# Attention scores of a sliding-window layer: a head's query stacked as high over low part in 128 rows, the key stored twice, two matrix products in place of three; and another order of the Vector engine's work at a group's last step

## The chip, the cores and the metric

One core of one Trainium2 chip runs the whole program. The metric is the device time of one execution in microseconds, from its first to its last instruction and the little that lies around them. Engines are named as in the profile: PE is the Tensor engine (PEld its weight loads), DVE the Vector engine, ACT the Scalar engine, POOL the GpSimd engine, SP the engine that issues the DMAs. Each works through a queue of its own in order, and they wait for each other by semaphores.

## What is computed

Two layers of a decoder trunk on 1024 tokens of width 1024, all in float32: layer 0 mixes by retention, layer 1 by sliding-window attention, and each is followed by a squared-ReLU MLP. The change touches the attention alone:

```python
q = rope(rmsnorm(q.reshape(b, s, 16, 64), q_gain), positions)     # 16 query heads
k = rope(rmsnorm(k.reshape(b, s, 4, 64), k_gain), positions)      # 4 key heads
kb = with_prev(k)      # per block of 128 queries: the block before and this one, 256 keys
scores = jnp.einsum("bnqkgd,bnskd->bnkgqs", qb, kb) * 64 ** -0.5
scores = jnp.where(mask, scores, -jnp.inf)
probs = softmax(concat([scores, sink]))[..., :-1]
o = jnp.einsum("bnkgqs,bnskd->bnqkgd", probs, vb)
return o.reshape(b, s, 16 * 64) @ w_out
```

## The kernel before

**Precision.** A float32 product is made of three fast ones. Each operand is split into a high part (a copy rounded to `float32r`, made on ACT) and a low part (operand minus high part, made on DVE), and `product` (lines 528 to 538) issues high x high, high x low and low x high. In the profile these three are L533, L534 and L535. A name with `_hi` or `_lo` is such a part.

**Order of the program.** Retention, its output projection, the MLP of layer 0, the attention (about 1.5 to 1.9 ms into the trace), and the MLP of layer 1. The order on every engine is written out by hand.

**The attention.** It is 4 groups (one key head and its four query heads each) of 8 steps (`TT`, one block of 128 tokens each), 32 steps. `sw_steps` writes for each engine what it does in a step `s` of a group `g`. Group 0 and group 3 are written out, groups 1 and 2 are the two turns of a hardware loop (`Fori`), and two draining steps follow. The block `i` passes through the stages in three successive steps:

- `a_pe`: projection of the block to 384 columns (256 query, 64 key, 64 value), 24 matmuls. ACT squares it (`sq_act`, L2274) and copies it (`copy_act`, L2281); DVE sums the squares (`var_dve`, L2394); POOL refines the reciprocal root (L516 to L526); DVE scales (`scale_dve`, L2406, L2412); POOL finishes the rotary turn (`rope_sw_pool`, L2438 to L2448), with the queries in `qr` and the key in `kr`.
- One step later: `b_pe` transposes queries and key to bank `SB` of the PSUM (L2211 to L2213). ACT makes the high parts (`qkT_act`, L2299, L2300), DVE the low ones (`qkT_dve`, L2332, L2333). `c_pe` makes the scores. DVE adds the mask (`mask_half`, L2352), takes the maximum (`max_dve`, L2361) and compares it with the sink (`sink_dve`, L2368 to L2372). ACT takes the exponentials (`exp_act`, L2315). DVE inverts the sum (`den_dve`, L2378, L2380). ACT and DVE scale two heads each (`prob_act`, L2291; `prob_dve`, L2454).
- One step later: `d_pe` transposes the probabilities (L2232, 8 transposes), ACT and DVE split them (L2307, L2339), `e_pe` multiplies with the values (12 matmuls), ACT and DVE split the output into `aT` (L2325, L2460).
- `f_pe`: two tiles of the output projection for each step, six steps late (`FLAG`), 12 matmuls, which `add` (L712) adds to the residual. Group 0 has no `f` before its seventh step.

The PE's order in a step is a, b, d, f, c, f, e; in the first step of groups 1 to 3 both f come ahead of a. ACT's is `sq`, `qkT`, `copy`, `pT`, the exponentials, `oT`, `prob`. DVE's is `qkT`, `vlo`, `var`, then a list `work` (the low parts of the probabilities, mask, maximum, sink), `scale`, the two `add`, `oT`, `den`, `prob`. At a group's last step (`s == TT - 1`, not in the last group) ACT and DVE also split the next group's projection weights (`ws_hi`, `ws_lo`), and `a_pe` of the next step waits for all four `ws_lo`. There `work` is: low parts, one add, the two masks, one split, one add, three splits; the maxima and the sink follow behind `scale`.

**The scores before.** The transposed query of two heads `2j` and `2j + 1` fills 128 rows. The key has 64 rows, and is kept in two forms, `e = 0` with zeros below and `e = 1` with zeros above it (`kr` has 3 blocks of 64 columns, the outer ones zero, and two transposes of it give both). So a matmul of 128 rows by `2 x 2 x 128 = 512` columns gives the scores of two heads with 256 keys, and half of the rows that it multiplies are zeros.

## Time and profile before

| | |
|---|---|
| time, median of 3 executions | 2551.59 us (2548.61 to 6429.32) |
| the profiled execution | 2549.4 us, its span 2547.6 us |
| granted TensorE clock, mean | 0.99 of full speed |
| PE busy | 2485.4 us, 98% |
| PE weight loads | 2082.0 us, 82% |
| DVE busy | 1801.8 us, 71% |
| ACT busy | 1011.0 us, 40% |
| POOL busy | 341.8 us, 13% |

The page's row of 40 equal slices shows PE at 9 tenths or more nearly everywhere; the exceptions are the first slice (7) and slices 24 and 25 (8 and 8, about 1465 to 1592 us), where the attention begins. Busy time on PE is the time in which some matmul is in flight. It doesn't tell whether a matmul could have been left out without anything changing; for that one asks what the chain of waits runs through. Numbers in brackets at the end of a row of the timeline are the idle time of the engine ahead of the instruction and what ended it.

### The profile page before, as it was taken

To read this page: it belongs to the slowest core of one execution; us is meant where nothing else is said; L and a number is where in the kernel's file an instruction comes from. 1 tells how busy PE (TensorE), PEld (TensorE's weight loads), DVE (VectorE), ACT (ScalarE), POOL (GpSimd) and SP (SyncE) were. 2 spreads that over 40 slices of the span, in tenths; PEclk is the share of its full clock that TensorE was granted. 3 is DMA by queue.
4 is the path that set the end of the run, shared out by engine and by line. 5 is a ranking of instruction groups with operands and counts; after the bars stand their busy time and mean duration, and the time that the engine had idled before them with its cause. 6 is when DMAs were issued, how large, how long until landed. Compare 5 with 4: busy or idle time off the path is not lost. (4 is left out here: it accounts for less than half of the span.)

```text
span 2547.6 us, 35354 instructions
## 1 busy us (share of the span) xinstructions
PE 2485.4 (98%) x11593; PEld 2082.0 (82%) x11593; DVE 1801.8 (71%) x3095; ACT 1011.0 (40%) x1816; POOL 341.8 (13%) x667
## 2 busy tenths in 40 slices
PE   7999999999999999999999988999999999999999
PEld 6888888888788888888888877889877888888887
DVE  6545445454478877777877778888888777787775
ACT  6222222322323444443333345555555444333332
POOL 2102011021000300000000055444441000000000
PEclk9999999999999999999999999999999999999999
DMA  6112021120161334438344111011014344554403
GB/s 208 35 50 75 18 62 59 50 79 13 64 255 33 124 109 165 173 120 322 135 166 149 50 32 40 9 37 41 12 65 135 136 150 173 214 215 166 166 33 99
DMA packets 195069, 269.80 MB, mean 106 GB/s; under 512 B 22225, under 2 KB 104433, under 8 KB 194930
## 3 DMA queue, kind: packets, MB, share of 16 engines
q1 hardware_dynamic: 192626, 263.85, 30.3%
q10 hardware_dynamic: 2304, 4.20, 0.4%
q8 instruction: 75, 1.23, 0.2%
q14 instruction: 64, 0.52, 0.1%
HBM read 190.41 MB, written 77.60 MB: 105 GB/s over the span
## 5 line engine op out<-in xcount | busy, mean ns | idle before, releaser
L533 PE MATMUL ps<-bh,uw_hi 128*128 128x512 f32 x880 | 343.4, 390 | 4.9 <-DVE uw_lo L867 2.3
L534 PE MATMUL ps<-bl,uw_hi 128*128 128x512 f32 x880 | 342.9, 390 | 0.0
L535 PE MATMUL ps<-bh,uw_lo 128*128 128x512 f32 x880 | 342.9, 390 | 0.0
L533 PE MATMUL ps<-opB_hi,opA_hi 128*128 128x512 f32 x784 | 305.0, 389 | 0.0
L534 PE MATMUL ps<-opB_lo,opA_hi 128*128 128x512 f32 x784 | 305.0, 389 | 0.0
L535 PE MATMUL ps<-opB_hi,opA_lo 128*128 128x512 f32 x784 | 305.0, 389 | 0.0
L712 DVE TENSOR_TENSOR xT<-ps,xT 128x512 f32<-128x512 f32 x256 | 173.2, 687 | 83.7 <-PE ps L535 83.4
L533 PE MATMUL ps<-aT_hi,wd_hi 128*128 128x512 f32 x512 | 204.4, 399 | 4.1 <-DVE wd_lo L483 4.1
L534 PE MATMUL ps<-aT_lo,wd_hi 128*128 128x512 f32 x512 | 200.9, 392 | 0.0
L535 PE MATMUL ps<-aT_hi,wd_lo 128*128 128x512 f32 x512 | 200.9, 392 | 0.0
L533 PEld LDWEIGHTS ps<-bh,uw_hi 128*128 128x128 f32 x880 | 165.6, 188 | 40.7 <-issue 6.3
L1444 DVE TENSOR_TENSOR xT<-ps,xT 128x512 f32<-128x512 f32 x196 | 131.5, 685 | 94.1 <-PE ps L535 94.1
L534 PEld LDWEIGHTS ps<-bl,uw_hi 128*128 128x128 f32 x880 | 165.6, 188 | 34.2
L535 PEld LDWEIGHTS ps<-bh,uw_lo 128*128 128x128 f32 x880 | 165.4, 188 | 34.4
L535 PEld LDWEIGHTS ps<-opB_hi,opA_lo 128*128 128x128 f32 x784 | 147.1, 188 | 30.7
L534 PEld LDWEIGHTS ps<-opB_lo,opA_hi 128*128 128x128 f32 x784 | 147.1, 188 | 30.6
L533 PEld LDWEIGHTS ps<-opB_hi,opA_hi 128*128 128x128 f32 x784 | 147.1, 188 | 30.4
L1919 DVE BATCH_NORM_STATS2 bn<-ps 128x6 f32<-128x512 f32 x32 | 22.3, 698 | 181.2 <-PE ps L535 181.2
L1426 ACT ACTIVATE opA_hi<-blkA 128x1024 fp32r<-128x1024 f32 x60 | 63.1, 1051 | 183.8 <-PE ps L535 181.3
L2315 ACT ACTIVATE xn<-xn,nmax 128x256 f32<-128x256 f32 x128 | 63.6, 498 | 136.8 <-DVE sdif L2372 136.8
L533 PEld LDWEIGHTS ps<-aT_hi,wd_hi 128*128 128x128 f32 x512 | 97.1, 190 | 23.3 <-issue 4.5
L535 PEld LDWEIGHTS ps<-aT_hi,wd_lo 128*128 128x128 f32 x512 | 97.0, 189 | 20.7
(327 smaller groups left out, 5654.8 us busy)
## 6 DMA issues: line engine op xcount, KB each, us to landing
blkB<-t_dram SPq DMA_DIRECT2D x42, 1024.0 KB, 5.5
raw<-in_w_up SPq DMA_DIRECT2D x64, 512.0 KB, 4.7
raw<-in_ret_w_in SPq DMA_DIRECT2D x48, 512.0 KB, 4.9
blkA<-in_w_down SPq DMA_DIRECT2D x24, 1024.0 KB, 7.6
t_dram<-xn SPq DMA_DIRECT2D x72, 256.0 KB, 2.0
xT<-x_dram SPq DMA_DIRECT2D x24, 512.0 KB, 6.5
t_dram<-h SPq DMA_DIRECT2D x48, 256.0 KB, 2.1
y_dram<-xn SPq DMA_DIRECT2D x32, 256.0 KB, 2.3
```

The source lines that it names most:

```text
L533: pe.matmul(bank, ah, bh, start=(begin and i == 0), stop=False, skip_group_check=not begin)
L534: pe.matmul(bank, ah, bl, start=False, stop=False, skip_group_check=not begin)
L535: last = pe.matmul(bank, al, bh, start=False, stop=(i == len(pairs) - 1), skip_group_check=not begin)
L712: dve.tensor_tensor(xT[:, k, cols], ps[:, banks[m % len(banks)], :], xT[:, k, cols], ALU.add).then_inc(x_add, 1)
L1426: act.activation(op_hi[side, (n + 1) % 2][:, piece_of(h), :], part(layer, name, h), ACT.Copy).then_inc(op_hi_s, 1)
L1444: dve.tensor_tensor(dst, ps[:, op_bank(n, m), :], dst, ALU.add).then_inc(op_add, 1)
L1919: dve.bn_stats(bn[:], ps[:, BO, :]).then_inc(stats, 1)
L2315: act.activation(prob[:, hh, :, :], prob[:, hh, :, :], ACT.Exp, bias=nmax[:, hh:hh + 1], accum_out=ssum[:, hh:hh + 1]).then_inc(sw_exp, 1)
```

## The change

- **Scores.** One tile `qT` of 128 rows takes the place of `qT_hi` and `qT_lo`. `qT[:, e, j, :]` holds one head: for `e = 0` its high part in rows 0 to 63 and its low part in rows 64 to 127, for `e = 1` the other way round. The key is stored twice, in rows 0 to 63 and again in rows 64 to 127, without zeros. One matmul with the key's high part then gives high x high plus low x high, and a second with its low part the rest; each has 256 columns. The low x low product comes on top.
- **ACT and DVE.** The query's high part and its low part are made by two instructions of 64 rows each in place of one of 128 rows. The two DVE instructions read rows 0 to 63 and write rows 64 to 127, and the other way round. The key's parts have 128 columns in place of 256.
- **POOL.** The key's rotary turn is computed for two copies (128 and 64 columns in place of 64 and 32). `kr` needs no zeros, and one `memset` goes.
- **PE.** Three transposes in `b_pe` in place of four.
- **Order.** At a group's last step the maxima and the sink come ahead of the splits of the next group's weights.

```diff
@@ -2209,17 +2208,18 @@
             for j in range(2):
                 pe.transpose(ps[:, SB, j * P:(j + 1) * P], qr[:, j * P:(j + 1) * P], ident[:])
-            pe.transpose(ps[:, SB, 2 * P:3 * P], krf[:, SW_DH:3 * SW_DH], ident[:])
-            pe.transpose(ps[:, SB, 3 * P:4 * P], krf[:, 0:2 * SW_DH], ident[:]).then_inc(b_mm, 1)
+            pe.transpose(ps[:, SB, 2 * P:3 * P], krf, ident[:]).then_inc(b_mm, 1)
 
         def c_pe(pe, g, t):
             i = TT * g + t
             pe.wait_ge(sw_qlo, 2 * (i + 1))
             for j in range(2):
                 wait(pe, sw_masked, 2 * (i - 1) + j + 1)
-                product(pe, ps[:, SS + j, :],
-                        [(qT_hi[:, j, :], qT_lo[:, j, :], kT_hi[:].rearrange("p e s n -> p (e s n)"),
-                          kT_lo[:].rearrange("p e s n -> p (e s n)"))]).then_inc(c_mm, 1)
+                for e in range(2):
+                    bank = ps[:, SS + j, 2 * P * e:2 * P * (e + 1)]
+                    pe.matmul(bank, qT[:, e, j, :], kT_hi[:].rearrange("p s n -> p (s n)"), start=True, stop=False)
+                    last = pe.matmul(bank, qT[:, e, j, :], kT_lo[:].rearrange("p s n -> p (s n)"), start=False, stop=True)
+                last.then_inc(c_mm, 1)
 
@@ -2291,13 +2291,19 @@
+        def q_rows(e):
+
+            return slice(SW_DH * e, SW_DH * (e + 1))
+
         def qkT_act(act, g, t):
             i = TT * g + t
             act.wait_ge(b_mm, i + 1)
             wait(act, c_mm, 2 * i)
             tr = ps[:, SB, :].rearrange("p (j n) -> p j n", n=P)
-            act.activation(qT_hi[:], tr[:, 0:2, :], ACT.Copy).then_inc(sw_qhi, 1)
-            act.activation(kT_hi[:, :, t % 2, :], tr[:, 2:4, :], ACT.Copy).then_inc(sw_qhi, 1)
+            for e in range(2):
+                last = act.activation(qT[q_rows(e), e, :, :], tr[q_rows(e), 0:2, :], ACT.Copy)
+            last.then_inc(sw_qhi, 1)
+            act.activation(kT_hi[:, t % 2, :], tr[:, 2, :], ACT.Copy).then_inc(sw_qhi, 1)
 
@@ -2329,8 +2335,11 @@
             dve.wait_ge(sw_qhi, 2 * i + 2)
-            dve.tensor_tensor(qT_lo[:], tr[:, 0:2, :], qT_hi[:].bitcast(F32), ALU.subtract).then_inc(sw_qlo, 1)
-            dve.tensor_tensor(kT_lo[:, :, t % 2, :], tr[:, 2:4, :], kT_hi[:, :, t % 2, :].bitcast(F32),
+            for e in range(2):
+                last = dve.tensor_tensor(qT[q_rows(1 - e), e, :, :], tr[q_rows(e), 0:2, :],
+                                         qT[q_rows(e), e, :, :].bitcast(F32), ALU.subtract)
+            last.then_inc(sw_qlo, 1)
+            dve.tensor_tensor(kT_lo[:, t % 2, :], tr[:, 2, :], kT_hi[:, t % 2, :].bitcast(F32),
                               ALU.subtract).then_inc(sw_qlo, 1)
 
@@ -2434,18 +2443,19 @@
-            pool.tensor_tensor(k3, x4[:, nq], coss[:, t, :].unsqueeze(1).to_broadcast([P, 2, h]),
+            pool.tensor_tensor(k3, x4[:, nq].unsqueeze(1).to_broadcast([P, 2, 2, h]),
+                               coss[:, t, :].unsqueeze(1).unsqueeze(1).to_broadcast([P, 2, 2, h]),
                                ALU.mult).then_inc(sw_rcos, 1)
@@ -2675,8 +2685,8 @@
                     scores = softmax(g, s)
                     if s == TT - 1 and not last_group:
                         splits = [lambda j=j: sw_split_lo(eng, g + 1, j) for j in range(4)]
-                        work = lows(g, s) + outs[:1] + scores[:2] + splits[:1] + outs[1:] + splits[1:]
-                        outs = []
+                        work = lows(g, s) + outs[:1] + scores + splits[:1] + outs[1:] + splits[1:]
+                        outs, scores = [], scores[:2]
                     else:
                         work = lows(g, s) + scores
```

The first place is PE's `c_pe` in a step of group 1 to 2. Before, the scores of a block are:

```order
L533 MATMUL ps<-kT_hi,qT_hi 128x512
L534 MATMUL ps<-kT_lo,qT_hi 128x512
L535 MATMUL ps<-kT_hi,qT_lo 128x512
L134 REGISTER_ALU
L533 MATMUL ps<-kT_hi,qT_hi 128x512
L534 MATMUL ps<-kT_lo,qT_hi 128x512
L535 MATMUL ps<-kT_hi,qT_lo 128x512
```

And of the changed kernel (here of the written-out group 3):

```order
L2220 MATMUL ps<-kT_hi,qT 128x256
L2221 MATMUL ps<-kT_lo,qT 128x256
L2220 MATMUL ps<-kT_hi,qT 128x256
L2221 MATMUL ps<-kT_lo,qT 128x256
L2220 MATMUL ps<-kT_hi,qT 128x256
L2221 MATMUL ps<-kT_lo,qT 128x256
L2220 MATMUL ps<-kT_hi,qT 128x256
L2221 MATMUL ps<-kT_lo,qT 128x256
```

Six matmuls of 512 columns became eight of 256. The second place is what ACT does between a block's probabilities and its next copy, before:

```order
L2291 ACTIVATE xn<-xn,rden 128x256 x2
L2274 ACTIVATE scr<-ps,rstd 128x320
L2299 ACTIVATE qT_hi<-ps 128x256
L2300 ACTIVATE kT_hi<-ps 128x2x128
L2281 ACTIVATE qk_raw<-ps,rstd 128x320
```

and of the changed kernel:

```order
L2291 ACTIVATE xn<-xn,rden 128x256 x2
L2274 ACTIVATE scr<-ps,rstd 128x320
L2304 ACTIVATE qT<-ps 64x256 x2
L2306 ACTIVATE kT_hi<-ps 128x128
L2281 ACTIVATE qk_raw<-ps,rstd 128x320
```

One more instruction stands there, and the last one is half as long. The third place is DVE at the last step of group 1 and 2 (`ws_lo` are the next group's weights), before:

```order
L2352 SCALAR_TENSOR_TENSOR xn<-ps,swmask 128x512 x2
L2176 TENSOR_TENSOR ws_lo<-raw,ws_hi 128x8x128
L712 TENSOR_TENSOR xT<-ps,xT 128x512
L2176 TENSOR_TENSOR ws_lo<-raw,ws_hi 128x8x128
L2176 TENSOR_TENSOR ws_lo<-raw,ws_hi 128x8x64
L2176 TENSOR_TENSOR ws_lo<-raw,ws_hi 128x8x64
L2406 TENSOR_TENSOR scr<-qk_raw,hrs 128x320
L2412 TENSOR_TENSOR scr<-scr,sins 128x320
L2361 TENSOR_REDUCE smax<-xn 128x2 x2
L2368 TENSOR_TENSOR smax<-smax,sink_b 128x4
L2371 TENSOR_SCALAR nmax<-smax 128x4
L2372 TENSOR_TENSOR sdif<-sink_b,smax 128x4
```

and of the changed kernel:

```order
L2361 SCALAR_TENSOR_TENSOR xn<-ps,swmask 128x512 x2
L2370 TENSOR_REDUCE smax<-xn 128x2 x2
L2377 TENSOR_TENSOR smax<-smax,sink_b 128x4
L2380 TENSOR_SCALAR nmax<-smax 128x4
L2381 TENSOR_TENSOR sdif<-sink_b,smax 128x4
L2175 TENSOR_TENSOR ws_lo<-raw,ws_hi 128x8x128
L711 TENSOR_TENSOR xT<-ps,xT 128x512
L2175 TENSOR_TENSOR ws_lo<-raw,ws_hi 128x8x128
L2175 TENSOR_TENSOR ws_lo<-raw,ws_hi 128x8x64
L2175 TENSOR_TENSOR ws_lo<-raw,ws_hi 128x8x64
L2415 TENSOR_TENSOR scr<-qk_raw,hrs 128x320
L2421 TENSOR_TENSOR scr<-scr,sins 128x320
```

The two maxima and the sink's three small instructions moved ahead of four splits and an add.

## Rows read from the trace of the kernel before

**Rows 1.** Stretches: PE, PEld, DVE, ACT, POOL busy us (instructions), PEclk, DMA share, GB/s
```profile
1545.00:1579.00 34.00, 29.39 (x173) 25.84 (x174) 26.71 (x69) 20.30 (x62) 17.50 (x54) 1.00 0.12 32
1620.00:1680.00 60.00, 60.00 (x358) 55.38 (x357) 52.60 (x130) 36.59 (x110) 29.92 (x95) 1.00 0.11 28
```

**Rows 2.** Chain of waits in a steady stretch: start us, us, what
```profile
1726.50 0.40 ACT xn L2291
...
1728.35 0.31 DVE kT_lo L2333
...
1734.29 1.67 ACT xn L2315 x7
...
1737.53 0.39 ACT xn L2291
```

**Rows 3.** Timeline, PE, the same step: start us, us, engine, line, out<-in, count
```profile
1727.12 1.04 PE L2232 MATMUL ps<-ident,xn 128*128 128x128 f32 x8
...
1729.38 0.39 PE L533 MATMUL ps<-kT_hi,qT_hi 128*128 128x512 f32 x1
...
1729.61 0.39 PE L534 MATMUL ps<-kT_lo,qT_hi 128*128 128x512 f32 x1
...
1732.10 0.28 PE L533 MATMUL ps<-pT_hi,vp_hi 128*128 128x256 f32 x1
...
1732.21 0.28 PE L534 MATMUL ps<-pT_lo,vp_hi 128*128 128x256 f32 x1
```

**Rows 4.** Timeline, DVE, ACT and POOL, the same step
```profile
1728.01 0.42 DVE L2332 TENSOR_TENSOR qT_lo<-ps,qT_hi 128x256 fp32r<-128x256 f32 x1 [1.23 <-ACT kT_hi L2300]
...
1728.35 0.41 DVE L2333 TENSOR_TENSOR kT_lo<-ps,kT_hi 128x256 fp32r<-128x256 f32 x1
...
1728.72 0.28 DVE L2387 SCALAR_TENSOR_TENSOR vp_lo<-ps,rstd,vp_hi 128x64 fp32r<-128x64 f32 x1
...
1735.36 0.33 POOL L2440 TENSOR_TENSOR kr<-scr,coss 128x64 f32<-128x64 f32 x1
...
1735.76 0.46 POOL L2445 TENSOR_TENSOR scr<-scr 128x128 f32<-128x128 f32 x1
...
1736.81 0.26 POOL L2448 TENSOR_TENSOR kr<-kr,scr 128x32 f32<-128x32 f32 x1
...
1738.35 0.37 ACT L2299 ACTIVATE qT_hi<-ps 128x256 fp32r<-128x256 f32 x1
...
1738.62 0.38 ACT L2300 ACTIVATE kT_hi<-ps 128x256 fp32r<-128x256 f32 x1
```

**Rows 5.** Timeline, two steps of group 0 that have no output projection
```profile
1550.62 0.38 PE L533 MATMUL ps<-pT_hi,vp_hi 128*128 128x256 f32 x1 [0.55 <-DVE pT_lo L2339]
...
1556.67 0.91 ACT L2291 ACTIVATE xn<-xn,rden 128x256 f32<-128x256 f32 x2 [0.77 <-DVE rden L2380]
...
1567.65 0.91 ACT L2291 ACTIVATE xn<-xn,rden 128x256 f32<-128x256 f32 x2 [0.77 <-DVE rden L2380]
```

**Rows 6.** Timeline across the turn from group 1 to group 2
```profile
1675.75 0.42 DVE L2332 TENSOR_TENSOR qT_lo<-ps,qT_hi 128x256 fp32r<-128x256 f32 x1
...
1684.65 0.44 PE L533 MATMUL ps<-ws_hi,hT_hi 128*128 128x384 f32 x1 [0.45 <-DVE ws_lo L2176]
...
1685.44 1.27 DVE L2361 TENSOR_REDUCE smax<-xn 128x2 f32<-128x512 f32 x2
...
1687.37 1.27 DVE L712 TENSOR_TENSOR xT<-ps,xT 128x512 f32<-128x512 f32 x2
...
1691.94 1.09 PE L2232 MATMUL ps<-ident,xn 128*128 128x128 f32 x8 [2.42 <-ACT xn L2291]
...
1692.38 0.38 ACT L2300 ACTIVATE kT_hi<-ps 128x256 fp32r<-128x256 f32 x1
...
1694.35 0.43 DVE L2332 TENSOR_TENSOR qT_lo<-ps,qT_hi 128x256 fp32r<-128x256 f32 x1 [2.77 <-issue]
...
1695.25 0.79 PE L533 MATMUL ps<-kT_hi,qT_hi 128*128 128x512 f32 x1 [2.22 <-DVE kT_lo L2333]
```

More of the change, by code:

```diff
@@ L270, in trunk @@
             pT_lo = sb("pT_lo", [P, 2, 4, P], F32R, z)
-            kT_hi = sb("kT_hi", [P, 2, 2, P], F32R, z)
-            kT_lo = sb("kT_lo", [P, 2, 2, P], F32R, z)
-            qT_hi = sb("qT_hi", [P, 2, P], F32R, z)
-            qT_lo = sb("qT_lo", [P, 2, P], F32R, z)
+            kT_hi = sb("kT_hi", [P, 2, P], F32R, z)
+            kT_lo = sb("kT_lo", [P, 2, P], F32R, z)
+            qT = sb("qT", [P, 2, 2, P], F32R, z)
             swmask = sb("swmask", [P, 4, P], F32, z)
@@ L283, in trunk @@
             ws_lo = sb("ws_lo", [P, KT, SW_COLS], F32R, z)
-            kr = sb("kr", [P, 3, SW_DH], F32, z)
+            kr = sb("kr", [P, 2, SW_DH], F32, z)
             vp_hi = sb("vp_hi", [P, 9 * SW_DH], F32R, z)
@@ L2426, in rope_sw_pool @@
             if isinstance(g, int) and i == 0:
-                pool.wait_ge(sw_zero, 8)
+                pool.wait_ge(sw_zero, 7)
             rsqrt_rest(pool, sw_rsq, REST * i, hvar[:], hrs[:], htmp[:])
@@ L2436, in rope_sw_pool @@
             q4 = qr.rearrange("p (a e d) -> p a e d", e=2, d=h)
-            k3 = kr[:, 1, :].rearrange("p (e d) -> p e d", e=2)
+            k3 = kr[:].rearrange("p a (e d) -> p a e d", e=2)
             pool.tensor_tensor(q4, x4[:, 0:nq], coss[:, t, :].unsqueeze(1).unsqueeze(1).to_broadcast([P, nq, 2, h]),
                                ALU.mult)
-            pool.tensor_tensor(k3, x4[:, nq], coss[:, t, :].unsqueeze(1).to_broadcast([P, 2, h]),
+            pool.tensor_tensor(k3, x4[:, nq].unsqueeze(1).to_broadcast([P, 2, 2, h]),
+                               coss[:, t, :].unsqueeze(1).unsqueeze(1).to_broadcast([P, 2, 2, h]),
                                ALU.mult).then_inc(sw_rcos, 1)
@@ L2446, in rope_sw_pool @@
             pool.tensor_tensor(q4[:, :, 1, :], q4[:, :, 1, :], s4[:, 0:nq, 0, :], ALU.add)
-            pool.tensor_tensor(k3[:, 0, :], k3[:, 0, :], s4[:, nq, 1, :], ALU.subtract)
-            pool.tensor_tensor(k3[:, 1, :], k3[:, 1, :], s4[:, nq, 0, :], ALU.add).then_inc(sw_radd, 1)
+            pool.tensor_tensor(k3[:, :, 0, :], k3[:, :, 0, :], s4[:, nq, 1, :].unsqueeze(1).to_broadcast([P, 2, h]), ALU.subtract)
+            pool.tensor_tensor(k3[:, :, 1, :], k3[:, :, 1, :], s4[:, nq, 0, :].unsqueeze(1).to_broadcast([P, 2, h]), ALU.add).then_inc(sw_radd, 1)
         def prob_dve(dve, g, t):
@@ L2862, in _ @@
                 norm_act(act, m, TILES * (DG_SW - 1))
-            act.wait_ge(sw_zero, 5)
+            act.wait_ge(sw_zero, 4)
             sw_steps("act", act)
@@ L2957, in _ @@
             pool.wait_ge(down_mm, TILES * (DG_SW - 1))
-            for z in (kr, kT_hi, kT_lo, vp_hi, vp_lo):
+            for z in (kT_hi, kT_lo, vp_hi, vp_lo):
                 flat = z[:].rearrange({2: "p a -> p a", 3: "p a b -> p (a b)", 4: "p a b c -> p (a b c)"}[len(z.shape)])
-                pool.memset(flat if z is kr else flat.bitcast(F32), 0.0).then_inc(sw_zero, 1)
+                pool.memset(flat.bitcast(F32), 0.0).then_inc(sw_zero, 1)
             for j, c in enumerate(HCONST):
```

## The prediction

> **What bounds the kernel now.** I read the busy times of stretches first. In the middle of a group PE is busy 60.00 of 60.00 us at a granted clock of 1.00 [rows 1]. That looks like an attention that is bound by PE, and a change that takes matmuls away would pay in full. So I read the chain of waits over the same kind of step next [rows 2]. It doesn't touch PE. It goes from ACT's scaling of the probabilities (L2291) to the squares, to the key's high part, to DVE (L2333), along DVE to the maximum and the sink, to ACT's exponentials (L2315), back to DVE for the inverse of the sum, and to L2291 of the next step: 1726.50 to 1737.53, a step of 11.03 us. Both can hold at once, if PE's work of a step and this loop happen to be equally long.
>
> Which of the two is the limit when the other gets shorter is told by steps with less work on PE. Group 0 has no output projection in its first six steps, which is 12 matmuls of 512 columns less, and at 0.23 us from one to the next [rows 3] 2.8 us. There the scaling starts at 1556.67 and at 1567.65, each time behind 0.77 us of waiting for DVE's inverse, and PE waits too, 0.55 us for one of DVE's low parts in a step before them [rows 5]. So a step takes 10.98 us with 2.8 us less on PE. The loop over DVE and ACT needs 10.98 us, and PE needs about 11.03. They are 0.05 us apart. What matters of the change is then what it does to the loop, not to PE.
>
> **PE.** The scores are six matmuls of 512 columns, 0.23 us apart, 1.37 us; they become eight of 256 columns, and such matmuls with new weights each follow at 0.11 to 0.12 us [rows 3], 0.92 us. One transpose goes, and eight take 1.04 us [rows 3], so 0.12. PE needs 0.57 us less per step, 10.46. That is the gain which the loop hides.
>
> **ACT in the loop.** The query's high part becomes two instructions of the same 256 columns. Half the rows save nothing if time goes by columns; no row shows a 64-row instruction, and I take that. The next instruction starts 0.27 us after such a one [rows 4], so +0.27. The key's part has 128 columns less, 0.13 at 0.27 per 256, so its 0.38 us become 0.25. Sum +0.14; if a short instruction has a floor at the 0.28 to 0.33 that 64 columns take on DVE and POOL [rows 4], +0.2. I take +0.16.
>
> **DVE in the loop.** Here too one more instruction of 256 columns stands, and the key's loses 128 columns. The low parts follow each other at 0.34 us (1728.01 to 1728.35) although the first lasts 0.42 [rows 4], so they overlap by 0.08. With that overlap kept the price is 0.34 - 0.13 = +0.21. The new instructions write other rows than they read, and no row of this trace does that. If the second query instruction and the key's behind it start only after the end of the one before, each loses the 0.08 and a start of about 0.02, which makes +0.41. I take the middle, +0.31.
>
> The Trainium skill has a rule that speaks for the upper end, in "VectorE: DVE Perf Modes", section "Two Vector instructions with no wait between them": an instruction whose inputs or output start in another quarter of the rows than those of the last one is held until all earlier ones have finished. No run here shows it so far. By it both instructions would be held.
>
> **The loop after.** 10.98 + 0.16 + 0.31 = 11.45 us (11.32 to 11.60). Before, a step is 11.03, so the change costs +0.42 per steady step (+0.3 to +0.57). These are steps 1 to 6 of groups 1 to 3, 18 in all: +7.6 us (5.4 to 10.3). In group 0 four steps go at the loop's own pace: 4 x 0.47 = +1.9.
>
> **POOL.** The key's product goes from 0.33 us (64 columns) to the 0.46 of 128 columns [rows 4], and each of the two last instructions from 0.26 (32 columns) to 0.33 (64): +0.27. What hides it: POOL ends at 1737.07 (1736.81 + 0.26), and the query's high part on ACT starts at 1738.35 [rows 4]; between them lie the transposes of `b_pe`, 0.6 us with the semaphores. That leaves about 0.65 us, and since ACT comes later by about the same 0.31 of DVE, it covers 0.27. Were it gone, each step would cost up to 0.27 more. At the very start, where the chain does run over POOL, I take +0.5 in all. The memset that goes stands once ahead of the attention and saves under 1 us off the path; I take 0.
>
> **The turns.** At steps 7 of groups 0 to 2 the maxima and the sink, 1.93 us (1685.44 to 1687.37), now stand ahead of the four splits that PE waits for at 1684.65 [rows 6]. So `a_pe` of the next group starts 1.93 + 0.31 = 2.2 us later, at 1686.9. Queued behind it on PE are b, d and c, and ACT's squares wait for it. Its 24 matmuls of 384 columns, at 0.23 us per 512, are 0.17 us apart, so it ends at about 1691.2; the squares (320 columns, 0.4), two query parts (0.54) and the key's (0.25) give 1692.5. Before, the key's high part ends at 1692.76 [rows 6], held up by the late exponentials. So the move exchanges one lateness for another: the exponentials come earlier by four splits, an add and the scaling, between 4 and 5 us, the projection comes 2.2 us later, and 0.2 us are left as a gain. At the hardware loop's own turn (one of three) DVE stood still for 2.77 us with nothing to wait for after its last work and started at 1694.35 [rows 6]; its last work ends earlier now, by the time it waited for the exponentials, an estimated 1 to 1.5 us, so that turn gains up to 1.8. Sum -2.2 us for the three.
>
> Against that stands TensorE's clock. After idle times of 2.42 and 2.22 us the matmul at 1695.25 takes 0.79 us, where the same takes 0.39 elsewhere [rows 3, 6]: the lower level, 1.2 GHz. It falls on c and e, which nothing waits for. After the change PE idles ahead of `a_pe`, some 2.4 us for the bank that the later add frees, and 0.9 us for the splits, and then a slow stretch lies on `a_pe` itself, on the path. Its 24 matmuls take 4.1 us at the upper level, 2.4 GHz; if three or four microseconds go at the lower level, each turn loses 1.7 us, 5.1 in all. I take the middle of -2.2 and +2.9, rounded to +0.5.
>
> **Sum.** 7.6 + 1.9 + 0.5 + 0.5 = +10.5 us. The profiled execution was 2549.4 us, which gives 2559.9. The runs' median is 2551.59, 2.2 above it, which gives 2562. I predict 2561 us, 0.4% slower.
>
> **Rivals.**
> 1. *PE is the limit, the change pays.* For it: 60.00 of 60.00 us busy [rows 1], and waits for PE nowhere exclude it. Against: the chain [rows 2] and the steps without a projection [rows 5]. It would need the extra instructions on ACT and DVE to cost nothing, for instance by overlapping fully with half the rows each, and 10.98 us would still allow only 0.05 us per step. If my reading of the loop is wrong altogether, the gain is 18 x 0.57 = 10 us and some 3 at the turns: 2549.4 + 2.2 - 13 = 2538 us. Chance 0.10.
> 2. *DVE's instructions do not overlap.* The upper end of above: 18 x 0.52 + 4 x 0.57 + 0.5 and 1.4 for the turns, +13.5 us, 2565 us. Chance 0.2. The Trainium skill's rule on held Vector instructions, cited above, is this case.
> 3. *The clock falls in the steady steps.* PE will idle 1.0 of 11.45 us per step. If that brought the lower level for good, PE would need twice 10.46 us, +9.5 us over 22 steps, +209 us: 2761 us. It decides from 51 us (2%), that is 2 us in each of 25 steps, for which PE must lose 3.0 us per step, 6 us of 11.45 at the lower level. Against it: in 1545 to 1579 us PE was busy for 29.39 of 34.00 us, less than it will be, and the granted clock was 1.00 [rows 1]. Chance 0.02.
> 4. *Gains at the turns and losses in the steps cancel*, with all bounds at their lower end (+5.4 + 1.4 + 0 - 4): about 2553 us. Chance 0.05.
>
> **How the numbers follow.** My own case has 0.63, with a range of 2555 to 2569. With rival 2 and the upper part of rival 4 the range 2550 to 2570 holds 8 in 10; rival 1 stays out. The measurement can tell about 2% (51 us) from no change. All cases but the third end within it: faster by over 2% 0.01, within 2% 0.96, slower 0.03.
>
> **What the profile after would show.** The start-to-start time of DVE's two query instructions: 0.34 or 0.43 us. The step, from one scaling of the probabilities to the next, in the middle of a group: 11.4 to 11.5 us; PE with about 1 us idle in it, waiting for ACT's L2291 or POOL. A chain of waits that still runs over ACT and DVE alone. At the turns a wait of PE for `ws_lo` or for the add, and whether `a_pe`'s matmuls go 0.17 or 0.32 us apart. I'm wrong if the step comes out at 10.5 to 10.9 us, which would say that the loop has slack that I don't see.

## The result and the profile after

| | before | after |
|---|---|---|
| time, median | 2551.50 us (2548.61 to 6429.32, 4 executions) | 2570.99 us (2570.44 to 2574.95, 4 executions) |
| ratio after / before, 95% interval | | 1.0091 (1.0078 to 1.0104) |
| the profiled execution, its span | 2549.4, 2547.6 us | 2574.95, 2573.1 us |
| PE busy | 2485.4 us, 98% | 2489.2 us, 97% |
| DVE busy | 1801.8 us, 71% | 1812.0 us, 70% |
| ACT busy | 1011.0 us, 40% | 1023.2 us, 40% |
| POOL busy | 341.8 us, 13% | 350.5 us, 14% |

The changed kernel is slower: 19.5 us lie between these two medians, and the ratio, which leaves out the one execution of 6429 us, says 0.9%, 20 to 27 us. The sign is that of the forecast, the size isn't: +9 us was forecast, to 2561, and the measured time lies 1 us above 2570, the upper end of the wider of the two ranges given. The profiled execution of after lies 4 us above its median and that of before 2 us below its own, so the two traces are 25.5 us apart, and those 25.5 us are what the readings below divide.

The page of after, its head, its busy times and its row of the granted clock in 40 slices:

```profile
span 2573.1 us, 35481 instructions
...
PE 2489.2 (97%) x11625; PEld 2076.7 (81%) x11625; DVE 1812.0 (70%) x3127; ACT 1023.2 (40%) x1848; POOL 350.5 (14%) x666
...
PEclk9999999999999999999999988999989999999999
```

PE was given fewer columns and is busy for 3.8 us longer: by this number alone a reader would not know that work was taken from it. The stretches of [rows 1] in the trace of after (columns as there) tell more:

```profile
1545.00:1579.00 34.00, 28.68 (x148) 27.08 (x147) 21.10 (x55) 18.49 (x57) 15.12 (x41) 0.78 0.12 32
1620.00:1680.00 60.00, 57.08 (x344) 49.98 (x343) 50.24 (x126) 33.55 (x104) 29.03 (x88) 1.00 0.07 19
```

In the middle of a group PE now idles for 2.9 of 60 us, at the full clock, and every engine is busy for less of the time. In group 0 the granted clock fell to 0.78, where before it was 1.00.

**The steady step.** The chain of waits in a steady stretch, start us, us, what:

```profile
1752.67 0.49 ACT xn L2291
...
1754.26 0.29 ACT kT_hi L2306
...
1755.46 0.29 DVE kT_lo L2342
...
1761.23 1.67 ACT xn L2321 x7
...
1764.45 0.49 ACT xn L2291
```

It runs through the same stations as [rows 2], over ACT and DVE and never over PE, and takes 1764.45 - 1752.67 = 11.78 us in place of 11.03. The timeline of ACT and DVE shows where the 0.75 us went:

```profile
1753.48 0.76 ACT L2304 ACTIVATE qT<-ps 64x256 fp32r<-64x256 f32 x2
...
1754.26 0.28 ACT L2306 ACTIVATE kT_hi<-ps 128x128 fp32r<-128x128 f32 x1
...
1754.57 0.86 DVE L2339 TENSOR_TENSOR qT<-ps,qT 64x256 fp32r<-64x256 f32 x2 [1.52 <-ACT kT_hi L2306]
...
1755.46 0.29 DVE L2342 TENSOR_TENSOR kT_lo<-ps,kT_hi 128x128 fp32r<-128x128 f32 x1
...
1755.67 0.27 DVE L2396 SCALAR_TENSOR_TENSOR vp_lo<-ps,rstd,vp_hi 128x64 fp32r<-128x64 f32 x1
```

ACT: two query parts in 0.78 us, then 0.28 for the key, 1.06 us; before 0.27 + 0.38 = 0.65 [rows 4]. That is +0.41. DVE: 1755.67 - 1754.57 = 1.10 us from the first query part to the instruction behind the key's; before 1728.72 - 1728.01 = 0.71 [rows 4]. That is +0.39. And 10.98 + 0.41 + 0.39 = 11.78.

**The whole attention.** I measure between starts of `b_pe` of successive steps. Its 31 intervals sum to 366.90 us before and 391.56 after, +24.7:

| stretch | before | after | more |
|---|---|---|---|
| group 0, six intervals | 70.86 | 79.11 | +8.25 |
| three stretches of six steady intervals | 66.33, 66.37, 66.69 | 70.72, 70.59, 70.67 | +12.6 |
| three turns, two intervals each | 28.86, 29.98, 27.45 | 29.10, 30.39, 29.25 | +2.45 |
| the last interval | 10.36 | 11.73 | +1.4 |

**Group 0.** Three of its intervals are 13.70, 13.54 and 13.59 us; before they were 12.10, 10.47 and 10.97. The timeline of PE in one of them:

```profile
1562.13 0.38 PE L2210 MATMUL ps<-ident,scr 128*128 128x128 f32 x2
...
1565.09 0.38 PE L2220 MATMUL ps<-kT_hi,qT 128*128 128x256 f32 x1 [1.59 <-DVE kT_lo L2342]
...
1567.27 0.58 PE L532 MATMUL ps<-pT_hi,vp_hi 128*128 128x256 f32 x1 [0.97 <-DVE pT_lo L2348]
...
1567.86 0.41 PE L534 MATMUL ps<-pT_hi,vp_lo 128*128 128x256 f32 x1
1568.08 0.41 PE L532 MATMUL ps<-pT_hi,vp_hi 128*128 128x256 f32 x1
...
1570.32 0.52 PE L533 MATMUL ps<-ws_lo,hT_hi 128*128 128x384 f32 x1
1570.63 0.52 PE L534 MATMUL ps<-ws_hi,hT_lo 128*128 128x384 f32 x1
...
1573.64 0.34 PE L532 MATMUL ps<-ws_hi,hT_hi 128*128 128x384 f32 x1
1573.81 0.33 PE L533 MATMUL ps<-ws_lo,hT_hi 128*128 128x384 f32 x1
...
1575.72 0.38 PE L2210 MATMUL ps<-ident,scr 128*128 128x128 f32 x2
```

PE stands still for 1.59 and 0.97 us. Behind that the matmuls of `e_pe` (256 columns) follow at 0.21 to 0.22 us in place of 0.12, and the first of `a_pe` (384 columns) at 0.31 to 0.32 in place of 0.17: the lower level, 1.2 GHz, from 1567 to 1573 us. These matmuls stand in a chain of their own here. `b_pe` of a block waits behind `a_pe` of the next in PE's queue, ACT and DVE turn its result into `kT_lo` 2.9 us later, `c_pe` waits for that, and behind `c_pe` stand e and a again. The trace's record of the granted clock agrees. Its mean from 1536 to 1577 us is 0.75, but that mean hides three stretches of 6.8 us, one in each of these steps (they start at 1539.3, 1552.9 and 1566.6 us), at 0.50, the lower level, and 1.00 between them. The third of them:

```profile
1566.60:1573.40 6.80, 6.13 (x23) 6.13 (x24) 5.05 (x15) 2.53 (x11) 4.31 (x14) 0.50 0.01 2
```

### The profile page after: what moved, and what is told of

Same layout as the page of the kernel before. It is cut to its first block and busy times, and to the rows that moved or that the text cites. A ratio compares the mean times of both kernels' runs of the same rounds, so it can differ in the third digit from the quotient of the medians.

```text
span 2573.1 us, 35481 instructions
## 1 busy us (share of the span) xinstructions
PE 2489.2 (97%) x11625; PEld 2076.7 (81%) x11625; DVE 1812.0 (70%) x3127; ACT 1023.2 (40%) x1848; POOL 350.5 (14%) x666
```

## The experiments

The runs of the kernel before that stand beside them have medians of 2549.0 to 2549.9 us.

### The order alone

The kernel before, with the maxima and the sink first at a group's last step.

```diff
-                        work = lows(g, s) + outs[:1] + scores[:2] + splits[:1] + outs[1:] + splits[1:]
-                        outs = []
+                        work = lows(g, s) + outs[:1] + scores + splits[:1] + outs[1:] + splits[1:]
+                        outs, scores = [], scores[:2]
```

> The kernel before with the new order at a group's last step alone (maxima and sink ahead of the splits of the next group's weights). My theory, by the sum of the prediction: a_pe of the next group starts about 1.9 us later, the exponentials 4 to 5 us earlier, and the three turns together cost between -2 us (TensorE at its upper level during a_pe) and +3 us (lower level). The steady steps stay at 11.02 us. In all 2549 to 2555 us. The rival, that the order is what made the changed kernel slow, expects at least half of its loss here: 2561 us or more, with the turns' 14.5 us grown to 17 us as in the changed kernel and not given back in the step behind.

Measured: 2544.56 us against 2549.02, ratio 0.9985 (0.9975 to 0.9994). The order alone is a gain of about 4 us, more than the 2 us that I had allowed for at most. The turns take 27.08, 27.58 and 26.55 us (before 28.86, 29.98, 27.45), together -5.1. PE and DVE at the turn from group 1 to 2, which answer to [rows 6], and one row of ACT ahead of it:

```profile
1684.63 0.45 PE L533 MATMUL ps<-ws_hi,hT_hi 128*128 128x384 f32 x1 [0.68 <-DVE ws_lo L2176]
...
1690.91 0.42 DVE L2332 TENSOR_TENSOR qT_lo<-ps,qT_hi 128x256 fp32r<-128x256 f32 x1 [2.60 <-ACT kT_hi L2300]
...
1691.80 0.49 PE L533 MATMUL ps<-kT_hi,qT_hi 128*128 128x512 f32 x1 [1.40 <-DVE kT_lo L2333]
```

```profile
1672.17 0.91 ACT L2291 ACTIVATE xn<-xn,rden 128x256 f32<-128x256 f32 x2 [0.80 <-DVE rden L2380]
```

The last ACT scaling ahead of the turn (this row) starts at 1672.17 here and at 1673.84 before, so the times compare from there. `a_pe` comes 12.46 us behind it, before 10.81: 1.65 us later, where 1.93 was forecast (the 2.2 less the 0.31 that is not in this kernel). DVE's `qT_lo` comes 18.74 us behind it, before 20.51, so 1.77 us earlier.

The row of `qT_lo` names ACT as what it waited for, but ACT's key was done at 1690.31, 0.6 us before it. The chain of waits shows what held DVE, first in the kernel before, then here (`DVEq` is DVE's sequencer; line 2716 is the hardware loop, whose turn ends there):

```profile
1691.04 3.16 issue
```

```profile
1687.76 3.00 issue
...
1690.76 0.10 DVEq L2716
```

So the standstill of [rows 6] is not gone. DVE stands still for 3.0 us behind the loop's branch in both kernels; it reaches the branch 1.6 us earlier here. The other part of the gain lies behind `qT_lo`. Before, the granted clock was 0.50 at each of the three turns (from 1597.5 to 1604.3, 1693.0 to 1699.9 and 1788.6 to 1792.0 us), and here it is 1.00 from 1590 to 1800 us: the first matmul of `c_pe` takes 0.49 us in place of 0.79. Counted from one `b_pe` to `qT_lo` and from there to the next `b_pe`, the three turns gained 0.59 + 1.77 + 0.87 = 3.2 us in the first part and 1.19 + 0.63 + 0.02 = 1.8 us in the second.

### The scores alone

The changed kernel with the order of before, the diff above turned round.

> The changed kernel with the order of before at a group's last step. My theory: the steady step is 11.78 us as in the changed kernel (11.02 before), 18 of them make +13.7 us, the steps of group 0 without a projection stay at about 13.6 us where TensorE is at its lower level every other stretch, +8 us in the profiled execution, and the turns go back to about 14.5 + 0.8 us. In all 2565 to 2572 us. If instead the order were the cause, this kernel would be within 3 us of the kernel before.

Measured: 2577.6 us, ratio 1.0111 (1.0094 to 1.0128). The sign is as expected, the size 6 us above. The steady step is 11.78 us, as in the changed kernel. The attention takes 395.38 us by the starts of `b_pe`, 28.5 more than before: 12.4 in the steady stretches, 8.4 in group 0, 6.3 at the turns (30.74, 32.38, 29.47) and 1.4 at the end. The timeline of PE at the turn of group 1 to 2:

```profile
1708.32 1.96 PE L2232 MATMUL ps<-ident,xn 128*128 128x128 f32 x8 [2.48 <-ACT xn L2291]
...
1713.06 0.57 PE L2220 MATMUL ps<-kT_hi,qT 128*128 128x256 f32 x1 [2.77 <-DVE kT_lo L2342]
```

The eight transposes take 1.96 us where they take 1.09 elsewhere, and the first matmul of `c_pe` 0.57 in place of 0.38: the lower level again. The transposes themselves aren't on the path, for `c_pe` waits 2.77 us more behind them; but the chain of waits runs over the matmuls of `e_pe` from 1715.21 us on, which follow at 0.21 in place of 0.12, and these are. The two parts of the change add up: -4 for the order and +28 for the scores (1.11%) make +24, and the changed kernel's ratio gives +23 (it was measured against other executions of before, so 1 or 2 us mean nothing). So the whole loss is the scores', and the order gives part of it back.

### Two instructions in the same rows

The scores alone, with both instructions of a pair in the same rows. This leaves out the second head of each pair: its query is a copy of the first one's, with the same instructions, rows and columns otherwise.

```diff
-                last = act.activation(qT[q_rows(e), e, :, :], tr[q_rows(e), 0:2, :], ACT.Copy)
+                last = act.activation(qT[q_rows(0), e, :, :], tr[q_rows(0), 0:2, :], ACT.Copy)
...
-                last = dve.tensor_tensor(qT[q_rows(1 - e), e, :, :], tr[q_rows(e), 0:2, :],
-                                         qT[q_rows(e), e, :, :].bitcast(F32), ALU.subtract)
+                last = dve.tensor_tensor(qT[q_rows(1), e, :, :], tr[q_rows(0), 0:2, :],
+                                         qT[q_rows(0), e, :, :].bitcast(F32), ALU.subtract)
```

> As the run with the scores alone, but both of ACT's query instructions read and write rows 0 to 63, and both of DVE's read rows 0 to 63 and write rows 64 to 127, so that the second of a pair starts at the same rows as the first; the second head of a pair is a copy of the first, so this kernel leaves out half of the heads' scores. Number, width and waits of the instructions are the same. Theory A (an instruction that starts at other rows than the last one isn't overlapped with it): ACT's pair is 0.27 us apart and not 0.39, its key part follows at once, from 1.06 us to 0.82 us for the three; DVE's pair is 0.34 us apart and not 0.43; the key behind it, which starts at other rows, still waits. Steady step 11.78 - 0.24 - 0.09 = 11.45 us. Theory B (any further instruction of 64 rows costs its whole length): nothing changes, 11.78 us.

Measured: 2562.67 us, ratio 1.0056 (1.0035 to 1.0076); the steady step is 11.41 us. ACT and DVE in a steady step:

```profile
1745.75 0.63 ACT L2304 ACTIVATE qT<-ps 64x256 fp32r<-64x256 f32 x2
...
1746.28 0.27 ACT L2306 ACTIVATE kT_hi<-ps 128x128 fp32r<-128x128 f32 x1
...
1746.58 0.75 DVE L2339 TENSOR_TENSOR qT<-ps,qT 64x256 fp32r<-64x256 f32 x2 [1.25 <-ACT kT_hi L2306]
...
1747.35 0.29 DVE L2342 TENSOR_TENSOR kT_lo<-ps,kT_hi 128x128 fp32r<-128x128 f32 x1
```

On ACT the key follows 0.53 us behind the pair's start, in the changed kernel 0.78. On DVE it is 0.77 against 0.89. Together 0.37 us, and 11.78 - 0.37 = 11.41. So it is the change of the starting row that costs, not the number of instructions and not the 64 rows, and it costs more on ACT (0.25) than on DVE (0.12). On ACT the rows of what is read and of what is written change together; which of them holds the instruction isn't told apart. What remains on DVE fits too: the pair's instructions overlap now, but they write from row 64 and the key's writes from row 0, and it starts only at their end (0.34 + 0.43 = 0.77).

The time fell by 15 us, more than 18 x 0.37 = 6.7. Of the rest, 5.5 us are group 0 (its six intervals sum to 73.82 us in place of 79.28): with a shorter loop the steps there are 12.72, 11.97 and 11.08 us in place of 13.84, 13.61 and 13.62, and behind 1555.9 us the granted clock is 1.00 there. Another 2.6 us are the turns.

### PE with less work, nothing else changed

The kernel before without the product of the query's low part, which this kernel leaves out: two matmuls of 512 columns less per step, 0.46 us.

```diff
-                product(pe, ps[:, SS + j, :],
-                        [(qT_hi[:, j, :], qT_lo[:, j, :], kT_hi[:].rearrange("p e s n -> p (e s n)"),
-                          kT_lo[:].rearrange("p e s n -> p (e s n)"))]).then_inc(c_mm, 1)
+                bank = ps[:, SS + j, :]
+                pe.matmul(bank, qT_hi[:, j, :], kT_hi[:].rearrange("p e s n -> p (e s n)"), start=True, stop=False)
+                pe.matmul(bank, qT_hi[:, j, :], kT_lo[:].rearrange("p e s n -> p (e s n)"), start=False,
+                          stop=True).then_inc(c_mm, 1)
```

> The kernel before, and of the three products of the scores the one of the query's low part is left out (two matmuls of 512 columns less per step, 0.46 us of PE); everything on ACT, DVE and POOL stays. Theory (the loop over ACT and DVE sets the step as soon as PE is a little shorter): the step goes from 11.02 to 10.98 us, 18 steps give -0.7 us, in all within 2 us of the kernel before, with PE idle for 0.4 us in each step. The rival, that PE's work bounds the attention, expects 10.56 us per step and 8 to 10 us less in all.

Measured: 2549.91 us, ratio 0.9999 (0.9990 to 1.0009); the steady step stays at 11.02 us in groups 1 and 2 and is 10.98 in group 3. The stretch of [rows 1] in the middle of a group:

```profile
1620.00:1680.00 60.00, 58.70 (x346) 53.12 (x347) 52.20 (x129) 36.57 (x110) 29.58 (x93) 1.00 0.11 28
```

PE has idle time now and the kernel isn't faster: 60.00 of 60.00 us busy was no sign of a limit. The rival that PE bounds the kernel falls.

### Group 0 with PE filled

The changed kernel with nine more matmuls (of `ws_hi` with 512 columns, into a bank that nobody reads) behind `a_pe` in the early steps of group 0, to tell whether the lower clock there comes from PE's pauses.

```diff
+                    if begins and s < 6:
+                        if s > 3:
+                            eng.wait_ge(n_var, 5)
+                        for _ in range(9):
+                            eng.matmul(ps[:, 7, :], ws_hi[:, 0, 0:P], hT_hi[:, 0, 0:HALF], start=True, stop=True)
```

> The changed kernel with nine matmuls of 512 columns more behind a_pe in steps 2 to 5 of group 0, into a bank that nobody reads then. They add 2.1 us of work on PE per step where it waits. Theory (in these four steps PE's pauses bring its lower level, which makes a step 13.6 us long where the loop over ACT and DVE needs 11.8): granted clock 1.00 from 1545 us on and steps of 11.8 us, 4 to 6 us less than the changed kernel, about 2566 us. The rival (it is the loop itself that is 13.6 us long there) expects no gain or a loss of up to 8 us.

Measured: 2574.39 us, ratio 1.0100 (1.0084 to 1.0115), no gain. A stretch of group 0:

```profile
1550.00:1564.00 14.00, 11.53 (x73) 10.39 (x72) 9.65 (x25) 8.13 (x24) 6.24 (x19) 1.00 0.00 1
```

The clock is 1.00 from 1531 to 1568 us (then 0.50 until 1571.9), and the intervals are 13.16, 12.83, 12.25 and 11.46 us. But the matmuls stand ahead of `b_pe`, in the chain that sets the pace here, and so they cost about what the clock gives (an argument, not a measurement); and the lower level came back at the turn behind, on `a_pe` (19.90 and 18.09 us for the first two long intervals, 17.27 and 17.14 without them). This experiment settles nothing about the time.

So once more, with the matmuls in the two places where PE waits: six behind `d_pe`, four ahead of `e_pe`, in three steps.

```diff
+                    def fill(count):
+                        if begins and s in (2, 4, 5):
+                            if s > 3:
+                                eng.wait_ge(n_var, 5)
+                            for _ in range(count):
+                                eng.matmul(ps[:, 7, :], ws_hi[:, 0, 0:P], hT_hi[:, 0, 0:HALF], start=True, stop=True)
...
+                    fill(6)
...
+                    fill(4)
```

> The changed kernel with matmuls of 512 columns into a free bank where PE has its pauses, in steps 2, 4 and 5 of group 0: six behind d_pe (1.4 us, where PE waits 1.59 us for kT_lo) and four ahead of e_pe (0.9 us, where it waits 0.97 us for pT_lo). Nine of them behind a_pe made the steps no shorter than 12.3 to 13.2 us, also at a granted clock of 1.00, because they stand in the row b_pe, kT_lo, c, e, a_pe, b_pe; these here fill pauses and lengthen nothing by more than 0.1 us. Theory (the pauses bring the lower level, and the lower level makes the steps 13.6 us long): granted clock 1.00 there, steps of about 11.8 us, in all 4 to 6 us less than the changed kernel, 2565 to 2567 us. If the steps stay at 13 us or more with the clock at 1.00, the length is not the clock's doing.

The stretch 1556 to 1576 us, first of the changed kernel, then of this one:

```profile
1556.00:1576.00 20.00, 17.44 (x86) 16.93 (x85) 12.36 (x34) 9.82 (x33) 8.55 (x23) 0.74 0.21 53
```

```profile
1556.00:1576.00 20.00, 18.57 (x110) 15.61 (x109) 14.47 (x38) 13.21 (x42) 10.02 (x28) 1.00 0.18 53
```

And ACT's scaling of the probabilities in it:

```profile
1558.82 0.91 ACT L2291 ACTIVATE xn<-xn,rden 128x256 f32<-128x256 f32 x2 [0.77 <-DVE rden L2389]
...
1570.59 0.91 ACT L2291 ACTIVATE xn<-xn,rden 128x256 f32<-128x256 f32 x2 [0.77 <-DVE rden L2389]
...
1582.37 0.91 ACT L2291 ACTIVATE xn<-xn,rden 128x256 f32<-128x256 f32 x2 [0.77 <-DVE rden L2389]
```

11.77 and 11.78 us from one to the next: with the clock at 1.00 group 0 goes at the loop's own pace, and its six intervals take 74.83 us in place of 79.11. That the 13.6 us steps are the clock's is shown. But the median is 2572.09 us, ratio 1.0083 (1.0066 to 1.0100), which can't be told from the changed kernel's. The other three executions of the changed kernel were already 4 us shorter than the profiled one, with a mean granted clock of 0.990 to 0.992 in place of 0.988. By an estimate from these means they spent 10 to 20 us less at the lower level, and the three stretches of group 0 are 20 us. How much of group 0's loss stands in an ordinary execution stays open.

### The same saving on PE without a change of rows

If the loss is the rows', then another form that spares PE the zeros should keep the loop short: the key twice in 128 rows as in the changed kernel, but each head's three products as matmuls of 64 rows, head e in rows 64e to 64e + 63, the two heads into two banks. ACT and DVE then work on 128 rows in one instruction, as before. With the order of before:

```diff
+                for hi_q, hi_k in ((True, True), (True, False), (False, True)):
+                    for e in range(2):
+                        bank = ps[:, SS + e, 2 * P * j:2 * P * (j + 1)]
+                        qq = (qT_hi if hi_q else qT_lo)[q_rows(e), j, :]
+                        kk = (kT_hi if hi_k else kT_lo)[q_rows(e), :, :].rearrange("p s n -> p (s n)")
+                        last = pe.matmul(bank, qq, kk, start=hi_q and hi_k, stop=not hi_q)
...
+            act.activation(qT_hi[:], tr[:, 0:2, :], ACT.Copy).then_inc(sw_qhi, 1)
...
+            dve.tensor_tensor(qT_lo[:], tr[:, 0:2, :], qT_hi[:].bitcast(F32), ALU.subtract).then_inc(sw_qlo, 1)
```

> Another way to leave out the zeros: the query's parts are made by one instruction of 128 rows each as before, the key stands twice in 128 rows as in the changed kernel, and the scores are three products for each head, each a matmul of 64 rows and 256 columns, with the two heads of a pair on the upper and the lower rows of the array into two different banks. Order at the group's last step as before; the mask of the first pair waits until both pairs are done. Theory (the loop over ACT and DVE sets the step, and what counts is the length of their instructions): ACT's two are 0.27 + 0.28 where before they are 0.65, DVE's 0.34 + 0.21 where before 0.71, so the loop is 10.98 - 0.10 - 0.16 = 10.72 us. If the matmuls of the two heads run beside each other PE needs 11.03 - 0.12 - 0.7 = 10.2 us, if one after the other 10.9. Steady step 10.72 to 10.9 us, in all 2544 to 2550 us, not slower than before. The rival, that fewer rows or more matmuls cost PE or the waits more, expects 11.1 us and more per step.

Measured: 2547.53 us, ratio 0.9996 (0.9986 to 1.0006). The steady step is 10.87 us. The timeline of PE around the scores:

```profile
1643.53 0.40 PE L535 MATMUL ps<-aT_hi,wd_lo 128*128 128x512 f32 x1
1643.86 0.39 PE L2224 MATMUL ps<-kT_hi,qT_hi 64*128 64x256 f32 x2
1644.08 0.28 PE L2224 MATMUL ps<-kT_lo,qT_hi 64*128 64x256 f32 x2
1644.20 0.27 PE L2224 MATMUL ps<-kT_hi,qT_lo 64*128 64x256 f32 x2
...
1644.75 0.50 PE L533 MATMUL ps<-aT_hi,wd_hi 128*128 128x512 f32 x1
1645.09 0.40 PE L534 MATMUL ps<-aT_lo,wd_hi 128*128 128x512 f32 x1
```

Each row `x2` is two matmuls that run beside each other, one head in each half of the rows, and the next pair follows at 0.12 us, like a single matmul of 256 columns. With the new order on top:

> The scores by matmuls of 64 rows, two heads beside each other, together with the new order at a group's last step. The first alone gave 10.87 us per steady step and no change that could be measured, the second alone -4.5 us. If they add up: 2541 to 2545 us, -5 us against the kernel before.

Measured: 2543.31 us, ratio 0.9973 (0.9962 to 0.9984), turns of 27.00, 27.98 and 27.44 us. And with DVE's sum of squares ahead of the value's low part, which was to take 0.16 us out of the loop:

```diff
+                        var_dve(eng, g, s)
                         vlo_dve(eng, g, s)
-                        var_dve(eng, g, s)
```

> The same with DVE's sum of squares (var_dve) ahead of the value's low part (vlo_dve) in the steps that are not the first ones. In the trace of the 64-row kernel DVE started the value's low part 0.37 us behind the key's, where 0.21 would do: it waits for ACT's vp_hi, 0.16 us, in the loop. With the sum of squares there instead the step is 10.87 - 0.16 = 10.7 us if the loop sets it, 20 steps give -3 us against the run without this: 2538 to 2542 us. If PE sets it (0.17 us between a_pe and b_pe, no wait) nothing changes.

Measured: 2541.24 us, ratio 0.9966 (0.9952 to 0.9979), 8 us less than before and 30 less than the changed kernel: the lowest median of all, though its executions (2537.97 to 2543.66) cover those of the run without the swap (2541.17 to 2543.99). Its steady step remained at 10.87 us, so the part of the expectation that was about the step failed. The swap didn't shorten the loop: the low parts of the probabilities start 1.70 us behind `qT_lo` in both kernels (1734.91 to 1736.61 here, 1735.31 to 1737.01 without the swap), because the value's low part still stands ahead of them in DVE's queue.

What sets 10.87 us in these kernels? The timeline shows PE without a pause, but a busy PE has told nothing once already. The steps of group 0 that have 2.8 us less work on PE, the same from which the prediction read 10.98, take 10.86 us here (10.85 with the swap). So the loop over ACT and DVE alone accounts for the step; whether PE has time to spare in it, no run here tests.

## Why the prediction was right and where it was wrong

**The loop, not PE: right.** The reading from group 0 [rows 5] that ACT and DVE need 10.98 us and PE 11.03 held. Taking 0.46 us from PE alone changed nothing, and the changed kernel's chain runs over ACT and DVE in every steady step.

**PE: right, and hidden.** The eight matmuls take 0.12 us each. PE waits in every step, for the loop.

**ACT in the loop: mis-sized, the main miss of the steady steps.** The step of the working that failed is "The next instruction starts 0.27 us after such a one, so +0.27". That row [rows 4] is of two instructions in the same rows. With other rows they follow at 0.39, and so does the key's behind them. I put +0.14 to +0.2 and it was +0.41. For DVE I had asked whether a change of rows undoes the overlap, and not for ACT, although its pair changes rows in the same way. 0.41 less the 0.16 of the sum, 0.25 us in each of 18 steps, is 4.5 us.

**DVE in the loop: rival 2's value.** +0.39, near the upper end of 0.21 to 0.41; I took the middle. The two query parts start 0.43 us apart, not 0.34. The Trainium skill, "VectorE: DVE Perf Modes", section "Two Vector instructions with no wait between them", says that an instruction that starts in another quarter of the rows than the last one, in what it reads or in what it writes, is held until all earlier ones have finished. The runs agree: 0.43 us apart with other rows, 0.34 with the same, and in that run too a wait ahead of the key's instruction, which writes from another row. No row of before could show it, and the mechanism was named; to give it 0.2 was too little. It is 18 x 0.08 = 1.4 us.

**The steady steps together:** 11.78 where 11.45 was forecast, 12.6 us in place of 7.6 in the stretches measured.

**POOL: right.** The instructions went from 0.33 to 0.47 us and from 0.26 to 0.32, +0.26 in all, and PE's wait ahead of `b_pe` is 0.33 us in a step that is 0.75 longer.

```profile
1764.41 0.43 PE L2210 MATMUL ps<-ident,scr 128*128 128x128 f32 x2 [0.33 <-POOL kr L2458]
```

This `b_pe` starts 0.13 us behind the last POOL instruction's end (1763.96 + 0.32), and ACT scales until 1764.94, so its cover is thin but there.

**Group 0: the lower clock, wrongly left to a rival of 0.02.** Forecast 1.9 + 0.5 us; +8.25 in the profiled execution. Rival 3 asked what it would cost if the lower level came in all steps, and excluded it with the stretch of before that had the same busy time and a clock of 1.00 [rows 1]. It came in three steps: a stretch's busy share of before didn't tell it. The kernel with the pauses filled shows that it is the clock, with 1.8 us per step of 13.6: there the six intervals of group 0 are 4.0 us longer than before, with the clock's part they are 8.25.

**The turns: the right exchange, and a lower level on the path that was put at nothing.** The order alone brought -5.1 where -2.2 was my lower bound. 3.2 us of it are the exchange that was forecast, with 1.77 at the loop's own turn (forecast: up to 1.8, by DVE's earlier last work). The other 1.8 us stand where the lower level is gone. The step that failed is "It falls on c and e, which nothing waits for": in the kernel before the chain of waits at this turn goes on over `c_pe` at 1695.25, and at the first turn over `c_pe`, `e_pe` and the start of `a_pe`, all at 0.50. At the third turn it doesn't touch the slow matmuls, and there this part gained only 0.02. With the order alone `a_pe` stayed at the upper level, which I had put at up to +5.1. In the changed kernel one stretch at 0.50, from 1798.7 to 1802.1 us, lies on the output projection and the first matmuls of `a_pe` ahead of the third turn, whose first interval is 17.79 us where the others are 17.28 and 17.14.

In the changed kernel the turns still cost +2.45. Its timeline at the turn from group 1 to 2, of ACT, PE and DVE:

```profile
1686.62 0.91 ACT L2291 ACTIVATE xn<-xn,rden 128x256 f32<-128x256 f32 x2 [0.78 <-DVE rden L2389]
...
1699.87 0.44 PE L532 MATMUL ps<-ws_hi,hT_hi 128*128 128x384 f32 x1 [0.68 <-DVE ws_lo L2175]
...
1705.36 0.53 ACT L2274 ACTIVATE scr<-ps,rstd 128x320 f32<-128x320 f32 x1 [1.86 <-issue]
...
1706.87 0.86 DVE L2339 TENSOR_TENSOR qT<-ps,qT 64x256 fp32r<-64x256 f32 x2 [3.59 <-ACT kT_hi L2306]
```

`a_pe` comes 13.25 us behind the last scaling ahead of the turn, 0.79 later than with the order alone: that is the 0.41 and 0.39 of the steady step. The squares on ACT (L2274) come 5.49 us behind `a_pe`, with the order alone 4.50. Here ACT too stands still at the hardware loop. Its sequencer's rows in the chain of waits (line 2726 is the loop):

```profile
1702.66 0.04 ACTq L2726
...
1705.18 0.05 ACTq L2726
```

From the branch's end to the first row of the next turn are 2.48 us; in the kernel before and with the order alone they are 0.20. With ACT's pair (+0.40), and DVE going at once behind the key where with the order alone it was still held (-0.67), DVE's query parts come 0.79 + 0.99 + 0.40 - 0.67 = 1.5 us later. ACT's standstill is 2.4 to 2.8 us in all five kernels whose ACT makes the query in two instructions, and 0.20 in the six that make it in one. From 1702.7 to 1705.2 us the changed kernel's trace has two DMA packets of the kind that brings in the program itself (queue, kind: packets, MB, share of 16 engines):

```profile
q14 instruction: 2, 0.02, 1.9%
```

That ACT waits for them is likely and isn't shown.

**The sum.** Steady +5.0 over the forecast, group 0 +5.8, turns +1.9, the last interval +1.4, together 14.1 of the 15.0 us by which the two traces' difference (25.5) exceeds the forecast (10.5). In the medians the miss is 10 us; the profiled executions add the rest. Rival 4, that all cancels, falls with the steady step. (Its -4 isn't the -2.2 that the turns had as their lower end, and its own terms give 2554 us, not 2553.)

## What to carry to other kernels

A busy share of 100% says nothing about a limit; the chain of waits and a stretch in which one engine has less to do do. Ahead of splitting one instruction into two, look at which rows each starts in, on ACT as much as on DVE, and where both lie in the loop that sets the step, take a form that keeps the rows (here matmuls of 64 rows side by side) instead. Work that is taken from PE below the pace of the loop becomes pauses, and these can bring the lower clock onto matmuls that are on the path.

## What the runs showed of the hardware

- **ACT too holds an instruction that starts in other rows.** Copies of 64 x 256 from PSUM follow at 0.39 us with a change of rows and at 0.27 without. On DVE it is 0.43 and 0.34. I had expected it of neither with certainty and of ACT not at all.
- **Matmuls of 64 rows in the two halves run beside each other**, a pair of 256 columns in 0.12 us. The change between them and matmuls of 128 rows costs about 0.2 us each way: into them 1643.86 - 1643.53 = 0.33 in place of 0.23 and then 0.22 in place of 0.12, out of them 0.20 in place of 0.12 and then 1645.09 - 1644.75 = 0.34 in place of 0.23.
- **The record of the granted clock and the spacing of the matmuls agree, if the stretch is cut finely enough.** Over 41 us of group 0 the mean is 0.75, a level that no matmul had: it is 0.50 from 1566.6 to 1573.4 us and 1.00 ahead of it, and the matmuls go at twice their usual spacing from 1567.6 to 1573.2.
- **DVE stands still at a hardware loop's turn**, 2.7 to 3.4 us in all eleven kernels here, and ACT 2.4 to 2.8 us in five of them and 0.20 in the other six. The idle time in brackets can name another engine for it; the sequencer's rows in the chain of waits show it.
- **Order and clock are tied.** In the kernel before, PE's pauses at the loop's turn (2.42 and 2.22 us) went with the lower level on c and e. With another order of DVE alone the pauses there are shorter (1.13, 0.68, 1.40 us), and the clock stays at 1.00.
